# Attention score maxima: 1024 columns at a time from one scratch tensor of two PSUM banks, in place of 512 at a time from a ring of two

## What is computed

```python
def blocked_attention(q, k, v):
    ...
    def one_block(qi):
        s = jnp.einsum('bqhgd,bkhd->bhgqk', qi.astype(F32), k.astype(F32))
        p = jax.nn.softmax(s, axis=-1)
        return jnp.einsum('bhgqk,bkhd->bqhgd', p, v.astype(F32))
```

## Time and profile before

| | |
|---|---|
| median of 3 runs | 4156.65 us |
| lowest, highest run | 4152.35, 4157.99 us |
| profiled execution: span from first to last instruction | 4152.1 us (no other time is given for it) |
| busy over the span | PE 89%, DVE 55%, ACT 37%, POOL 24% |
| mean granted clock of PE | 0.923 of full |

### The profile page before, as it was taken

The page is one execution under the profiler, slowest core; times in us unless marked ns, Lnnn a source line. Parts: engine busy times, 40 slices in busy tenths (PEclk is TensorE's granted clock), DMA queues, the critical chain, the costliest instruction groups (busy, mean ns, idle before and its releaser), DMA issues. The chain is left out here.

```text
span 4152.1 us, 49934 instructions
## 1 busy us (share of the span) xinstructions
PE 3710.2 (89%) x17410; PEld 3008.0 (72%) x17410; DVE 2277.6 (55%) x2717; ACT 1544.0 (37%) x1888; POOL 976.4 (24%) x510
## 2 busy tenths in 40 slices
PE   5886888888889879978786979999999999999998
PEld 2764665665666669966575867888888888888897
DVE  2776999999999941114475334334332433333264
ACT  2443665665556631126512432222221222222133
POOL 1553665666666610001121110000000000000000
PEclk8997999899989979986688989999999999999999
DMA  4332110011101022212354555334333433433374
GB/s 156 111 106 67 40 36 18 33 35 35 35 15 35 17 108 77 77 60 93 99 154 147 174 172 152 94 117 142 97 105 102 147 96 118 135 100 99 99 202 152
DMA packets 374863, 400.32 MB, mean 96 GB/s; under 512 B 37236, under 2 KB 282196, under 8 KB 374772
## 3 DMA queue, kind: packets, MB, share of 16 engines
q1 hardware_dynamic: 358568, 358.26, 27.8%
q0 software_dynamic: 8432, 31.46, 2.0%
q10 hardware_dynamic: 7776, 9.44, 0.7%
HBM read 318.02 MB, written 81.08 MB: 96 GB/s over the span
## 5 line engine op out<-in xcount | busy, mean ns | idle before, releaser
L783 POOL TENSOR_TENSOR att_acc<-att_acc,att_prob 128x1024 f32<-128x1024 f32 x224 | 618.3, 2760 | 311.0 <-ACT att_prob L938 304.7
L331 PE MATMUL ff_p<-ff_hhi,ff_whi 128*128 128x512 f32 (+1 forms) x1760 | 650.0, 369 | 33.8 <-DVE ff_hlo L1995 22.9
L999 DVE TENSOR_TENSOR att_tlo<-att_prob,att_thi 128x1024 fp32r<-128x1024 f32 x292 | 657.1, 2255 | 0.1
L1939 ACT ACTIVATE ff_whi<-ff_ws 128x2048 fp32r<-128x2048 f32 (+1 forms) x170 | 317.4, 1867 | 902.9 <-PE ff_p L333 885.8
L333 PE MATMUL ff_p<-ff_hhi,ff_wlo 128*128 128x512 f32 (+1 forms) x1760 | 649.3, 369 | 0.0
L332 PE MATMUL ff_p<-ff_hlo,ff_whi 128*128 128x512 f32 (+1 forms) x1760 | 649.2, 369 | 0.0
L1943 DVE TENSOR_TENSOR ff_wlo<-ff_ws,ff_whi 128x2048 fp32r<-128x2048 f32 (+1 forms) x170 | 378.4, 2226 | 386.3 <-ACT ff_whi L1939 386.0
L938 ACT ACTIVATE att_prob<-att_p_s 128x1024 f32<-128x1024 f32 x292 | 299.1, 1024 | 306.7 <-PE att_p_s L846 215.9
L331 PEld LDWEIGHTS ff_p<-ff_hhi,ff_whi 128*128 128x128 f32 x1760 | 333.7, 190 | 91.0 <-issue 36.0
L2023 DVE TENSOR_TENSOR ff_sil<-ff_sil,ff_p 128x512 f32<-128x512 f32 (+1 forms) x110 | 69.7, 634 | 587.4 <-PE ff_p L333 587.4
L1885 POOL TENSOR_TENSOR ff_rs<-ff_ms,neg_half 128x1 f32<-128x1 f32 x18 | 9.9, 552 | 1592.4 <-DVE ff_ms L2015 1592.4
(11 more groups left out here) (239 smaller groups left out, 6313.4 us busy)
## 6 DMA issues: line engine op xcount, KB each, us to landing
ff_ws<-in_w_ffn_dram SPq DMA_DIRECT2D x320, 512.0 KB, 4.8
att_aw<-in_ada_w_dram SPq DMA_DIRECT2D x8, 2048.0 KB, 8.0
proj_d<-gp_out SPq DMA_DIRECT2D x18, 784.0 KB, 4.0
hT_d<-qkv_hT SPq DMA_DIRECT2D x18, 512.0 KB, 2.8
qT_d<-qkv_qT SPq DMA_DIRECT2D x18, 512.0 KB, 2.9
att_qa<-qT_d SPq DMA_DIRECT2D x36, 256.0 KB, 2.8
gp_h<-hT_d SPq DMA_DIRECT2D x18, 512.0 KB, 4.8
qkT_d<-gs_qkT SPq DMA_DIRECT2D x18, 512.0 KB, 3.1
```

What stands on the lines that cost most here:

```text
L331: pe.matmul(out, ah, bh, start=first, stop=False)
L783: pool.tensor_tensor(e.sums, e.sums, prob[:, sl, :], ALU.add).then_inc(s.acc, 1)
L999: dve.tensor_tensor(tlo[:, sl, :], prob[:, sl, :], thi[:, sl, :].bitcast(F32), ALU.subtract).then_inc(s.lo, 1)
L1939: act.activation(whi[:, par, 0:cols], ws[:, par, 0:cols], ACT.Copy).then_inc(s.w_hi, 1)
```

## The change

`p_r` becomes one tensor of 1024 columns, two banks (`WIDE`). A piece is now two matmuls of 512 keys each, one into each bank, and one DVE reduction over 1024 columns; the cached keys of all four heads are one piece of four matmuls of 256. So a latent unit has 9 pieces and a context unit 1. `PLAN` gives two pieces to step 0 and one to each of the steps 1 to 7. `Walk.item` keeps one last use (`used`) in place of the ring of two: every user of `p_r` waits for the one directly before it. In step 8's turn, the row sums and the transposed sums only the first columns of the tensor are used. Lines shift by one at most.

```diff
--- before.py
+++ after.py
@@ -586,10 +586,11 @@
     ROW = 4 * P
     SLOTS_P = 6
     Q_SLOTS = 4
-    FULL = T_LAT // ROW
-    N_PIECES = G4 * FULL + G4 // 2
-
-    PLAN = [2, 2, 2, 3, 2, 3, 2, 2, 0]
+    WIDE = 2 * ROW
+    HALVES = T_LAT // WIDE
+    N_PIECES = G4 * HALVES + 1
+
+    PLAN = [2, 1, 1, 1, 1, 1, 1, 1, 0]
 
 
     CHUNKS = N_MOD * D_MODEL // 512 - MOD_FIRST
@@ -609,7 +610,7 @@
         ckp = ph.sb("ckp", [P, 2, KVH, 4, HD], F32R)
         qa = ph.sb("qa", [P, Q_SLOTS, ROW], F32R)
         qb = ph.sb("qb", [P, Q_SLOTS, ROW], F32R)
-        mx = ph.sb("mx", [P, 2, G4, FULL + 1])
+        mx = ph.sb("mx", [P, 2, G4, HALVES + 1])
         wm = ph.sb("wm", [P, 2, G4, P], F32R)
         prob = ph.sb("prob", [P, SLOTS_P, 2 * ROW])
         thi = ph.sb("thi", [P, SLOTS_P, 2 * ROW], F32R)
@@ -627,7 +628,7 @@
         mod = ph.sb("mod", [2, 512])
         ada_w = g.ada_w.rearrange("l (k p) n -> p (l k) n", p=P)
         p_s = [ph.ps("p_s0", 2 * ROW), ph.ps("p_s1", 2 * ROW)]
-        p_r = [ph.ps("p_r0"), ph.ps("p_r1")]
+        p_r = ph.ps("p_r", WIDE)
         p_o = [ph.ps("p_o0"), ph.ps("p_o1")]
 
         def unit(n, qt, kv, q, q_round):
@@ -636,7 +637,7 @@
             u.n, u.qt, u.kv, u.q, u.q_round = n, qt, kv, q, q_round
             if isinstance(n, int) and n >= L_UNITS:
                 m = n - L_UNITS
-                u.nds, u.kt0, u.pieces = NKC // 2, NKT, G4 // 2
+                u.nds, u.kt0, u.pieces = NKC // 2, NKT, 1
                 u.g0, u.p0, u.a0 = L_UNITS * NS + m, L_UNITS * N_PIECES + m * u.pieces, L_UNITS * (NS - 1) + m
                 u.step_no, u.sums, u.adds = [L_UNITS * NS + m], acc_ctx[:, m, :], 1
             else:
@@ -659,17 +660,15 @@
 
             def __init__(self, e=None, b=None, chunk=None):
                 self.chunk = chunk
-                self.index, self.fin, self.out, self.store, self.done, self.ring = 1, None, None, None, [None, None, None], [None, None]
+                self.fin, self.out, self.store, self.done, self.used = None, None, None, [None, None, None], None
                 if e is not None:
-                    self.index, self.done = 0, [(b, NS - 3), (b, NS - 2), (b, NS - 1)]
-                    self.ring = [(s.mx, e.p0 + N_PIECES), (s.aux, e.n + 1)]
+                    self.done = [(b, NS - 3), (b, NS - 2), (b, NS - 1)]
+                    self.used = (s.aux, e.n + 1)
 
             def item(self, sem, count):
 
-                bank, before = self.index % 2, self.ring[0]
-                self.index += 1
-                self.ring = [self.ring[1], (sem, count)]
-                return p_r[bank], before
+                before, self.used = self.used, (sem, count)
+                return p_r, before
 
             def pieces(self, v, i0, n):
                 return [(v, i, self.item(s.mx, v.p0 + (i + 1))) for i in range(i0, i0 + n)]
@@ -802,15 +801,16 @@
                         pe.wait_ge(s.q[v.q], v.q_round * 32 + 32)
                     if before:
                         pe.wait_ge(*before)
-                    if v.nds > 1 and i < G4 * FULL:
-                        h, c = i // FULL, i % FULL
-                        pe.matmul(bank[:, :], qa[:, v.q, h * P:(h + 1) * P], g.keysT[:, v.kv, 0, c * ROW:(c + 1) * ROW],
-                                  start=True, stop=True).then_inc(s.piece, 1)
+                    if v.nds > 1 and i < G4 * HALVES:
+                        h, c = i // HALVES, i % HALVES
+                        for n in range(2):
+                            last = pe.matmul(bank[:, n * ROW:(n + 1) * ROW], qa[:, v.q, h * P:(h + 1) * P],
+                                             g.keysT[:, v.kv, 0, c * WIDE + n * ROW:c * WIDE + (n + 1) * ROW], start=True, stop=True)
+                        last.then_inc(s.piece, 1)
                     else:
-                        h0 = 2 * (i - G4 * FULL if v.nds > 1 else i)
                         k0 = (v.kt0 + 2 * (v.nds - 1)) * P
-                        for n in range(2):
-                            last = pe.matmul(bank[:, n * 2 * P:(n + 1) * 2 * P], qa[:, v.q, (h0 + n) * P:(h0 + n + 1) * P],
+                        for h in range(G4):
+                            last = pe.matmul(bank[:, h * 2 * P:(h + 1) * 2 * P], qa[:, v.q, h * P:(h + 1) * P],
                                              g.keysT[:, v.kv, 0, k0:k0 + 2 * P], start=True, stop=True)
                         last.then_inc(s.piece, 1)
 
@@ -908,7 +908,7 @@
                     bank = item[0]
                     act.wait_ge(s.turn, v.n + 1)
                     wait(act, s.st, v.g0 - (NS if v.nds > 1 else 1))
-                    act.activation(qb[HD:P, v.q, :], bank[HD:P, :], ACT.Copy).then_inc(s.aux, 1)
+                    act.activation(qb[HD:P, v.q, :], bank[HD:P, 0:ROW], ACT.Copy).then_inc(s.aux, 1)
 
                 def step(S):
                     late = S.now and S.now[0].nds > 1
@@ -977,16 +977,15 @@
                     if i == 0:
                         wait(dve, s.nm, v.n - 1)
                     dve.wait_ge(s.piece, v.p0 + (i + 1))
-                    if v.nds > 1 and i < G4 * FULL:
-                        h, c = i // FULL, i % FULL
+                    if v.nds > 1 and i < G4 * HALVES:
+                        h, c = i // HALVES, i % HALVES
                         dve.tensor_reduce(mx[:, v.kv, h, c:c + 1], bank[:, :], AX.X, ALU.max).then_inc(s.mx, 1)
                     else:
-                        h0 = 2 * (i - G4 * FULL if v.nds > 1 else i)
-                        dve.tensor_reduce(mx[:, v.kv, h0:h0 + 2, FULL], bank[:, :].rearrange("p (h k) -> p h k", h=2), AX.X, ALU.max).then_inc(s.mx, 1)
+                        dve.tensor_reduce(mx[:, v.kv, :, HALVES], bank[:, :].rearrange("p (h k) -> p h k", h=G4), AX.X, ALU.max).then_inc(s.mx, 1)
                     if i == v.pieces - 1:
                         dve.wait_ge(s.mx, v.p0 + v.pieces)
                         wait(dve, s.turn, v.n - 1)
-                        parts = mx[:, v.kv, :, :] if v.nds > 1 else mx[:, v.kv, :, FULL:FULL + 1]
+                        parts = mx[:, v.kv, :, :] if v.nds > 1 else mx[:, v.kv, :, HALVES:HALVES + 1]
                         dve.tensor_reduce(wm[:, v.kv, :, HD], parts, AX.X, ALU.max).then_inc(s.nm, 1)
 
                 def step(S):
```

## The result

The changed kernel takes 4286.78 us (median of 4 runs, 4282.88 to 4288.74) against 4156.73 us (median of 4 as well); the ratio is 1.031, with a 95% interval of 1.0296 to 1.0324. The forecast was 4260 us, with a range of 4180 to 4330. The profiled execution has a span of 4287.2 us against 4152.1.

The account below looks back on a forecast made before the run. It took the attention as bound by a loop of waits between DVE, PE, ScalarE and POOL, not DVE work. Walk +66, start +8, context units +1 and clock +31 made +106; it took 4260 us, range 4180 to 4330.

Parts of the forecast that it names:

- The walk: One latent unit timed step by step at full clock: mean 35.8 us against 33.68, +66 us over 31 units.
- The clock term: Matmuls at PE's lower clock behind its stalls, half of their lateness reaching DVE: +1.0 us a unit, +31 us.
- The start: The first piece series, without cover, takes 22 us against 14: +8 us; context units at the end +1.
- The saving: Nine wide reductions replace 18 narrow ones per unit: 0.5 to 0.6 us less DVE work, under 20 us in all.
- The loop through the adds: POOL's adds hold the next `tlo` and so the next maximum; about 1.07 us of each `tlo` is not work.
- The three uncovered answers: In steps 0, 3 and 4 DVE idles for PE's two matmuls: about 0.85 us at full clock, 1.3 at lower.
- only the uncovered answers count: Rival, chance 0.17: late scores hide in steps 1 and 2; +0.9 us a unit, +37 with the start, about 4193.
- DVE work deciding: Rival, chance 0.08: DVE never idles for a piece, only the 0.6 us a unit saved remain, 4137 us.
- the port absorbing all: Rival, chance 0.05: idle DVE lets adds through that would have held `tlo`; unit stays at 33.7, 4157 us.
- a clock that stays low: Rival, chance 0.10: PE falls to the lower clock for good; +7 us a unit, 4380 us or so.
- The signs: Expected: DVE idle before maxima 3 us or more a unit, L807 wait over 120, stall 3 to 5, clock below 0.92.

Follow-up runs that it names:

- two_reductions: The changed kernel with each 1024-column piece reduced by two 512-column instructions, the semaphore raised by the second alone: 4289.67 us, ratio 1.0318 to the kernel before.
- wide_sums_out: The changed kernel with row sums and transposed sums moved to the output banks, a unit's first value matmul waiting for the reciprocal: 4282.77 us.
- wide_filled: The changed kernel with overwritten matmuls added in PE's idle time, 8 between step 0's pieces, 4 ahead of and 4 behind step 3's row sums: 4232.46 us.
- wide_plan_late: The changed kernel with the second piece moved from step 0 to step 6: 4230.62 us, ratio 1.0175 to the kernel before.
- ring_plan4: The kernel before, with its ring of two banks and 512-column reductions, but PLAN = [4, 2, 2, 2, 2, 2, 2, 2, 0]: 4215.19 us.

## Why the prediction was right, and where it wasn't

*The forecast* of slower, +103, was right in sign and place; +130 came. The walk's unit at full clock was 35.8 us; the kernel held near full clock (0.97) has 35.92. The walk's term of +66 measures as (35.92 - 33.68) x 31 = +69.

*The walk* came so close partly by luck. It gave 36.3 us for units with a chunk and 35.3 for those without; near full clock they take 38.13 and 33.70. One half was 1.8 us too short and the other 1.6 too long, and the mean hid it. The walk opens every unit with two held low parts, so that the first maximum starts at +5.65. In the trace only units with a chunk open so (1035.26 less 1029.88, +5.38). In those without, which follow a unit with one, it starts at +3.90 (1072.77 less 1068.87). The one unit read from the trace before was of the longer kind.

*The clock term* was the one mis-sized. I counted half of ten late matmuls, +1.0 us a unit, +31; it is 37.70 - 35.92 = 1.78 a unit, 54 us by the two medians. There are two such stretches in a unit, behind the stall of step 0 and behind the reciprocal, where I had counted ten late matmuls in all. In units without a chunk DVE stands waiting for just these matmuls and the full clock gives 2.6 us back; in those with one the added matmuls give 1.0.

*The start*: +8 expected; the first window maximum is at 391.85 against 384.57, +7.3. By the last window maximum of a latent unit the profiled execution is 130.2 behind, and the rest of the attention adds 4.6, where I had +1.

*The saving* of 0.5 to 0.6 us a unit was in the walk as work on the path. The duration was right (1220 ns against 1.21 us), its worth wasn't: in two_reductions 1 to 3 us reach the end, if any, where 18 were expected. The Trainium skill's rule on one large tile (VectorE: DVE Perf Modes, The TRN2 errata) holds for the instruction: by the rows above a wide maximum and what follows it are 1.14 us apart (1042.21, 1043.35), where two narrow ones took 1.20. That is half of the 0.125 us a pair worked out from the page, and it gains nothing where the engine waits for others.

*The loop through the adds* was right as a reading of `tlo`, and wrong as the mechanism of the loss: 3.61 of the 4.02 us a unit remain without it.

*The three uncovered answers* were all seen, with 0.83 us at the higher clock and 1.31 at the lower, as worked out (0.85 and 1.3). But the reason was incomplete: what PE has queued behind the answer counts too, the scores in step 0 and, by the traces of wide_sums_out and wide_filled, the values and scores of step 3, for which `att_oo` waits. The rival "only the uncovered answers count" (+37) falls with wide_plan_late, where their number is the same and 56 us are gone. DVE work deciding, the port absorbing all, and a clock that stays low are excluded by the times. The Trainium skill's advice to break up instructions where VectorE makes bubbles on other engines (Perfetto Trace Analysis, Optimizing Scalar/DVE Operations) holds here for the release only: two_reductions splits the instruction and not the release, and changes nothing; ring_plan4 splits both and is 74 us below it.

*The signs.* DVE's idle time before maxima went to 6.0 us a unit (185.9 over 31), PE's stall in step 0 is 4.13 us, the granted clock 0.88, all as announced. PE's wait at L807 for maxima went to 90.2 us, not over 120; with the waits there for the reciprocal it is 125.7, before 82.2.

Open stays how the +74 of the single last use divides between the steps; no kernel restored the ring for one of them alone. The traces of two_reductions and ring_plan4 give a first cut: of their 1.75 us a unit, 0.7 lie between window maximum and reciprocal and 1.1 behind it. A ring of two wide tensors, which would keep both, wasn't tried; it would take two banks more than the eight that `p_s`, `p_r` and `p_o` have now.

## What to carry to other kernels

Merging two buffers into one for a larger instruction trades a fixed cost of some 0.06 us for a hand-over of 0.8 us or more wherever no other work stands between two users: count these places first. Then look at what is queued behind the waiting instruction on the producer; here moving the second piece away from the scores took back 56 of 130 us. An engine that is 96% busy by the profile may have a third of that in waits; the least and the mean duration of a group, side by side, show it. In the changed kernel, shorter work on DVE bought at most 3 us. And where units take turns in two kinds, read one of each before working out a mean.

## What the runs showed of the hardware that I had not expected

Matmuls whose results are thrown away, put into PE's stalls, made the changed kernel 54 us faster: at 16 more per unit the mean granted clock between 600 and 1400 us went from 0.89 to 0.97. In the kernel before, eight more around the row sums gave 9 us, at the edge of what can be told.
